# A hybrid decoder step on one core: a different order of row-tile turns and squares ahead of the first products, and query latents on 520 columns

## The reference, cut to what matters

```python
xn = rmsnorm(h, g_norm)                       # 536 rows x 2048
proj = xn @ w_in                              # 2048 -> 4416
u, zs, cq, ckv, kpe, za = split(proj)         # 1024, 1024, 768, 512, 64, 1024
ssm_out = glu(gelu(ssm_scan(u) + d * u)) * silu(zs)
q = rmsnorm(cq, g_qn) @ w_uq                  # query latent -> 8 heads of 128 + 64
c, k_pe = rmsnorm(ckv, g_kvn), rope(kpe)      # stored for all 536 rows
o = attention(q, c, k_pe)                     # prompt: causal; samples: 2048 paged keys each
h = h + concat(ssm_out, o * silu(za)) @ w_out
y = rmsnorm(h, g_final)[16:]                  # the meta rows are dropped
```

## Time and profile before

| what | us |
|---|---|
| timed runs: lowest, median, highest | 1114.28, 1118.61, 1121.12 |
| the profiled execution | 1112.71 |
| its span, first to last instruction | 1111.0 |
| TensorE busy in it | 1040.4 (94%) |
| granted TensorE clock, mean over the span | 0.976 |

### The profile page before, as it was taken

One profiled execution on the slowest core, in us unless ns is written; L12 is line 12 of the kernel. 1 busy time (PEld: TensorE's weight loads), 2 busy tenths in 40 slices (PEclk: granted clock), 3 DMA queues, 4 the chain that ended last, 5 costly groups with the idle time before them and its releaser, 6 DMA issues.

```text
span 1111.0 us, 26974 instructions
## 1 busy us (share of the span) xinstructions
PE 1040.4 (94%) x10653; PEld 961.2 (87%) x10653; DVE 627.1 (56%) x1348; ACT 376.6 (34%) x783; POOL 159.0 (14%) x257
## 2 busy tenths in 40 slices
PE   6799999999999999999999989888799899999995
PEld 5699999999999999998899987665565569999995
DVE  5467264544286656659795527578789733323332
ACT  6521211122124221134652221455446423223333
POOL 0002230000050000010340720304344200000000
PEclk8799999999999999999999999889999999999998
DMA  9435843331353433243645774748998894332213
GB/s 258 102 99 128 168 122 91 96 96 52 96 163 105 136 102 114 86 141 98 218 140 155 235 227 155 229 152 259 288 296 283 265 299 130 91 98 76 80 34 154
DMA packets 201772, 169.90 MB, mean 153 GB/s; under 512 B 37547, under 2 KB 166054, under 8 KB 200102
## 3 DMA queue, kind: packets, MB, share of 16 engines
q1 hardware_dynamic: 178566, 119.12, 38.1%
q0 software_dynamic: 11616, 29.11, 8.7%
q10 hardware_dynamic: 11496, 20.36, 5.1%
HBM read 140.89 MB, written 25.31 MB: 150 GB/s over the span
## 4 chain that ended last, share of the span: by engine, by line
PE 80%; ACT 7%; DVE 4%; issue 4%; DMA 3%; SPq 1%; ACTq 0%; POOL 0%; DVEq 0%; POOLq 0%
PE gemm L2126 13%; PE gemm L2127 13%; PE gemm L2128 13%; PE gemm L2494 6%; PE gemm L2496 6%; PE gemm L2495 6%; PE misc L2398 2%; PE gemm L2413 2%; PE misc L2202 2%; PE gemm L2443 1%; PE misc L2212 1%; PE misc L2153 1%; PE gemm L2332 1%; PE gemm L2334 1%; PE gemm L2333 1%
## 5 line engine op out<-in xcount | busy, mean ns | idle before, releaser
L2126 PE MATMUL gemm<-xh,w_hi 128*128 128x260 f32 (+2 forms) x1056 | 302.2, 286 | 0.0
L2127 PE MATMUL gemm<-xl,w_hi 128*128 128x260 f32 (+2 forms) x1056 | 300.7, 285 | 0.0
L2128 PE MATMUL gemm<-xh,w_lo 128*128 128x260 f32 (+2 forms) x1056 | 299.9, 284 | 0.0
L1321 DVE TENSOR_TENSOR w_lo<-w_raw,w_hi 128x2048 fp32r<-128x2048 f32 (+3 forms) x63 | 110.6, 1756 | 159.1 <-ACT w_hi L861 157.1
L861 ACT ACTIVATE w_hi<-w_raw 128x2048 fp32r<-128x2048 f32 (+3 forms) x63 | 90.7, 1439 | 321.8 <-PE gemm L2128 280.5
L2126 PEld LDWEIGHTS gemm<-xh,w_hi 128*128 128x128 f32 x1056 | 198.8, 188 | 0.7
L2128 PEld LDWEIGHTS gemm<-xh,w_lo 128*128 128x128 f32 x1056 | 199.1, 189 | 0.0
L2127 PEld LDWEIGHTS gemm<-xl,w_hi 128*128 128x128 f32 x1056 | 198.9, 188 | 0.0
L2494 PE MATMUL gemm<-comb_hi,w_hi 128*128 128x260 f32 x512 | 147.7, 288 | 1.2 <-DVE comb_lo L1984 1.1
L2496 PE MATMUL gemm<-comb_hi,w_lo 128*128 128x260 f32 x512 | 145.5, 284 | 0.0
L2495 PE MATMUL gemm<-comb_lo,w_hi 128*128 128x260 f32 x512 | 145.5, 284 | 0.0
(11 more groups left out here) (397 smaller groups left out, 1994.1 us busy)
## 6 DMA issues: line engine op xcount, KB each, us to landing
w_raw<-w_in SPq DMA_DIRECT2D x35, 1024.0 KB, 6.3
ckv<-cache_ckv POOLq DMA_DIRECT2D x76, 256.0 KB, 3.8
w_raw<-w_out SPq DMA_DIRECT2D x16, 1024.0 KB, 5.8
ckv<-cache_ckv SPq DMA_DIRECT2D x52, 256.0 KB, 3.6
z_d<-ev ACTq DMA_DIRECT2D x16, 260.0 KB, 2.1
w_raw<-w_glu SPq DMA_DIRECT2D x8, 512.0 KB, 4.2
yt<-x_prompt SPq DMA_DIRECT2D x4, 1024.0 KB
o_y_p<-yt SPq DMA_DIRECT2D x4, 1024.0 KB
```

What stands on the lines that cost most here:

```text
L1321: dve.tensor_tensor(w_lo[:, slot, 0:width], w_raw[:, slot, 0:width], w_hi[:, slot, 0:width].bitcast(F32), ALU.subtract).then_inc(w_lo_read ...
L2126: pe.matmul(acc, a, xa, start=k == 0, stop=False)
L2127: pe.matmul(acc, a, xb, start=False, stop=False)
L2128: last = pe.matmul(acc, b, xa, start=False, stop=k == k_tiles - 1)
```

## The change

1. **Tile 4 on its own.** The 24 rows of tile 4 are loaded before tiles 2 and 3 and turned as one group (group 8) of sixteen small transposes into one bank. A new function `x_last` makes both parts on VectorE in three operations on 384 columns. Tiles 2 and 3 are groups 9 to 16, four k-tiles each; their high parts are made by ScalarE, the low parts by VectorE.
2. **Turns between products.** Groups 8 to 14 stand before k = 1, 3, ..., 13 of half 0 of block 1, groups 15 and 16 behind it. Half 1 of block 0 has no turns inside.
3. **Squares.** Tile 3 is squared by VectorE (one operation with a running sum, in place, after its last `xl`), tiles 2 and 4 by ScalarE after its last `xh`.
4. **Factors later.** The spreading products stand inside half 1 of block 1, between k = 5 and k = 6.
5. **Query latents on 520 columns.** The six query blocks of B_LAT use OWN; the copies, the stores, the load back, squares, sums, scaling and splits leave the 16 meta columns out. The loops of ScalarE and VectorE around them are cut in two or written out.
6. **Page groups 4 and 5** wait for gemm_done to reach B_V instead of B_K.

```diff
-X_GROUPS = [(t, k, 4) for t in range(3) for k in range(0, KD, 4)] + [(3, k, min(3, KD - k)) for k in range(0, KD, 3)]
+X_GROUPS = [(t, k) for t in (0, 1) for k in range(0, KD, 4)] + [(4, 0)] + [(t, k) for t in (2, 3) for k in range(0, KD, 4)]
+X_DONE = [4 * g + 4 if g < 8 else 4 * g + 3 for g in range(len(X_GROUPS))]
...
+            sp.dma_start(xtok[0:N_META, 4, :], x_prompt[4 * P - N_META:SEQ, :]).then_inc(x_loaded[2], 16)
+            sp.dma_start(xtok[N_META:N_META + N_SAMPLE, 4, :], x_sample).then_inc(x_loaded[2], 16)
             for t in (2, 3):
...
-            pool.wait_ge(gemm_done, B_K)
+            pool.wait_ge(gemm_done, B_V)
             for i in (4, 5):
                 load_pages(pool, i, (0, 1), 0)
...
-            square(0)
-            square(1)
-            act.wait_ge(xh_done, 48)
-            x_high(range(12, len(X_GROUPS)))
-            for t in (2, 3, 4):
-                square(t)
+            square(0, 0)
+            square(1, 1)
+            x_high(range(9, 17))
+            square(2, 2)
+            square(4, 3)
...
+            def x_last():
+                rows = TILES[4][1]
+                turned = misc[0][:, 0:KD * rows].rearrange("p (k t) -> p k t", k=KD)
+                gain = vecs[:, GN:GN + KD].unsqueeze(2).to_broadcast([P, KD, rows])
+                dve.wait_ge(xt_ready, 9)
+                dve.tensor_tensor(turned, turned, gain, ALU.mult).then_inc(xl_done, 1)
+                dve.wait_ge(xl_done, 33)
+                dve.tensor_copy(xh[:, :, 4 * P:T], turned).then_inc(xl_done, 1)
+                dve.wait_ge(xl_done, 34)
+                dve.tensor_tensor(xl[:, :, 4 * P:T], turned, xh[:, :, 4 * P:T].bitcast(F32), ALU.subtract).then_inc(xl_done, 1)
...
-            x_low(range(8, 12), high_too=True)
-            x_low(range(12, len(X_GROUPS)))
+            x_last()
+            x_low(range(9, 17))
+            dve.scalar_tensor_tensor(out=xtok[:, 3], in0=xtok[:, 3], scalar=1.0, in1=xtok[:, 3], op0=ALU.mult, op1=ALU.mult,
+                                     accum_out=stat[:, 3:4]).then_inc(xl_done, 1)
...
-                for h, (h0, hw) in enumerate(HALVES):
+                    for h, (h0, hw) in enumerate(halves):
+            copy_query, copy_key = copy_out(OWN), copy_out(HALVES)
...
             pe.wait_ge(w_lo_ready, 2)
             for k in range(KD):
-                if k in (3, 6, 9, 12):
-                    turn_x((8 + (k - 3) // 3,))
+                if k % 2 and k < 15:
+                    turn_x((8 + k // 2,))
                 first_half(1, 1, 0, (k,))
-            turn_x(range(12, 16))
-            for k in range(KD):
-                if k in (3, 6):
-                    turn_x((16 + (k - 3) // 3,))
-                last = first_half(0, 0, 1, (k,), 3 * KD)
-            last.then_inc(gemm_done, 1)
-            pe.wait_ge(x_scaled, 5)
-            pe.wait_ge(xl_done, 4 * KD)
-            for t in range(5):
...
-            first_half(1, 1, 1, range(KD)).then_inc(gemm_done, 1)
+            turn_x((15, 16))
+            first_half(0, 0, 1, range(KD), 51).then_inc(gemm_done, 1)
+            first_half(1, 1, 1, range(0, 6))
+            spread_factors()
+            first_half(1, 1, 1, range(6, KD)).then_inc(gemm_done, 1)
...
-                multiply(n, n % 2, KD, xh, xl, lambda b=b: chunk_sums(b))
+                multiply(n, n % 2, KD, xh, xl, lambda b=b: chunk_sums(b), halves=OWN if b < 4 else HALVES)
```

More of the change, by code:

```diff
@@ L392, in blocks, with with_first_pass @@
                 body(n, n // 2, n % 2, n + 2 if n + 2 < B_OUT or B_OUT <= n < B_END - 2 else None)
-        def with_first_pass(eng, body, first_pass):
+        def with_first_pass(eng, body, late, first_pass):
             for n in (B_LAT, B_LAT + 1):
                 body(n, n // 2, n % 2, B_LAT)
[L398 to L403, removed]
+            for first in (0, 4):
+                with eng.Fori(0, 2) as i:
+                    for u in range(2):
+                        n = B_LAT + 2 + first + u
+                        first_pass(i * 2 + (first + u))
+                        (body if first == 0 else late)(i * 2 + n, i + n // 2, n % 2, B_LAT)
+            late(B_LAT + 10, (B_LAT + 10) // 2, B_LAT % 2, B_LAT)
         bias_glu = vecs[:, 10:18]
@@ L410, in build, with lat_cols @@
         KPE_OUT = (d["o_kpe_p"].rearrange("l b t r -> (l b t) r"), d["o_kpe_s"].rearrange("l b t r -> (l b t) r"))
+        def lat_cols(k):
+            return slice(N_META if k < 6 else 0, T)
         def gate_count(n, r, slot):
@@ L841, in _, with square @@
         def _(act):
-            def square(t):
+            def square(t, before):
                 rows = TILES[t][1]
@@ L1522, in _ @@
             for n in (B_LAT, B_LAT + 1):
[L1523 to L1524 removed]
+                copy_query(n, n // 2, n % 2, B_LAT)
+            with dve.Fori(0, 2) as i:
                 for u in range(2):
@@ L2052, in turn_x @@
                     else:
-                        pe.wait_ge(x_loaded[t], (32, 16, 16, 48)[t])
+                        pe.wait_ge(x_loaded[min(t, 6 - t)], (32, 16, 48, 16, 48)[t])
                     if g >= 4:
                         pe.wait_ge(xl_done, X_DONE[g - 4])
-                    for i in range(kw):
-                        cols = slice((k0 + i) * P, (k0 + i + 1) * P)
-                        last = pe.transpose(misc[g % 4][:, i * width:i * width + P], xtok[:, t, cols], ident[:])
-                        if t == 3:
-                            rows = width - P
-                            last = pe.transpose(misc[g % 4][:, i * width + P:(i + 1) * width], xtok[0:rows, 4, cols], ident[0:rows, 0:rows])
+                    rows = TILES[t][1]
+                    for i in range(KD if t == 4 else 4):
+                        last = pe.transpose(misc[g % 4][:, i * rows:(i + 1) * rows], xtok[0:rows, t, (k0 + i) * P:(k0 + i + 1) * P],
+                                            ident[0:rows, 0:rows])
                     last.then_inc(xt_ready, 1)
@@ L2073, in first_half, with spread_factors @@
                 return last
+            def spread_factors():
+                pe.wait_ge(x_scaled, 5)
+                for t in range(5):
+                    rows = TILES[t][1]
+                    out = misc[0][:, t * P:(t + 1) * P] if t < 4 else misc[1][:, 0:rows]
+                    last = pe.matmul(out, ones[0:rows, :], diag[0:rows, t, 0:rows], start=True, stop=True)
+                last.then_inc(prep_t_ready, 1)
             turn_x(range(0, 8))
@@ L2080, in _ @@
             for k in range(KD):
-                if k in (3, 6, 9, 12):
-                    turn_x((8 + (k - 3) // 3,))
+                if k % 2 and k < 15:
+                    turn_x((8 + k // 2,))
                 first_half(1, 1, 0, (k,))
-            turn_x(range(12, 16))
-            for k in range(KD):
-                if k in (3, 6):
-                    turn_x((16 + (k - 3) // 3,))
-                last = first_half(0, 0, 1, (k,), 3 * KD)
-            last.then_inc(gemm_done, 1)
-            pe.wait_ge(x_scaled, 5)
-            pe.wait_ge(xl_done, 4 * KD)
-            for t in range(5):
-                rows = TILES[t][1]
-                out = misc[0][:, t * P:(t + 1) * P] if t < 4 else misc[1][:, 0:rows]
-                last = pe.matmul(out, ones[0:rows, :], diag[0:rows, t, 0:rows], start=True, stop=True)
-            last.then_inc(prep_t_ready, 1)
-            first_half(1, 1, 1, range(KD)).then_inc(gemm_done, 1)
+            turn_x((15, 16))
[3 more added lines that the diff above has]
+            first_half(1, 1, 1, range(6, KD)).then_inc(gemm_done, 1)
             pe.wait_ge(prep_t_read, 3)
```

110 lines of the change are left out of this document (51 added, 59 removed).

## The result

| | before | after |
|---|---|---|
| timed runs, median us (lowest to highest) | 1116.81 (1114.28 to 1121.12) | 1096.88 (1094.34 to 1104.86) |
| the profiled execution, us | 1112.71 | 1097.7 |
| its span, us | 1111.0 | 1095.6 |

The ratio is 0.984 (95% interval 0.980 to 0.988), which is 17.8 us less; the two medians are 19.9 us apart. The median of 1096.88 us lies in the range of the forecast, 0.9 us above its lower end. The same kernel timed again later gave 1095.08 us against 1114.17 for the kernel before, 0.981 (0.978 to 0.985). Its two profiled executions took 1097.7 and 1096.9 us.

The account below looks back on a forecast made before the run. TensorE, busy 1040.4 of 1111.0 us, was taken as the bound, gains coming from its stalls, slow clock or columns. Gains 12.5 + 2.0 + 2.2 = 16.7 us: profiled 1112.7 to 1096.0, median 5.9 above, 1101.9; range 1096 to 1110.

Parts of the forecast that it names:

- a start without its slow clock and its long wait: From block 0, half 0 to block 2: 26.9 us instead of 39.41, so block 2 starts at 52.5, 12.5 us earlier.
- shorter query blocks: Query latents: six blocks go from 11.87 to 11.53 us each, 2.0 us gained.
- key weights without page loads beside them: Key blocks: the 6.11 us load takes about 3.06 and the idle 2.22 us goes; 2.2 us gained, bounds 0 to 3.05.
- the turn of four: Start, TensorE: four transposes of one group cost 0.44 us, eight such groups 3.52.
- the factors: Start: after the squares and a 3.41 us rest of the chain, the row factors are ready at 45.7.
- the wait for them: Before the spreading products: TensorE arrives at 44.6 and waits 1.1 us, where it waited 5.56.
- the spreading products: Inside half 1 of block 1: 1.28 us at the upper clock, half of 2.56; 2.56 if they don't follow the clock.
- the rival of the weights: Start: block 2 waits for its weights, or the factors are late; TensorE waits 1.5 to 2.4 us, 1103.9; chance 0.12.
- 0.6 us of cover, and more gain at the start would find this wait: Before block 2: its weights' load, high part, low part and copies are done at 51.9, against its start at 52.5.
- The rival with 0.15: Start: the clock falls between the turns, 7 us at half speed costing 3.5 us, up to 10; 1108.9; chance 0.15.
- wrong if a later stage waits for something that doesn't move with TensorE: Whole kernel: one sign of a wrong prediction; the other was a start gaining less than 8 us.
- 3.4 us of scatter: Range of the timed median: the runs shown differ by 6.8 us, so 3.4 was allowed to each side.

Follow-up runs that it names:

- loads-first kernels: Changed kernel, weight loads of blocks 2 and 3 ahead of the `cnat` loads, spreading at k = 9: 1095.31 us, 0.983; with page groups 4, 5 moved back: 1097.06, 0.986.
- pages only: Kernel before with one edit: page groups 4 and 5 wait for gemm_done to reach B_V instead of B_K; 1113.41 us, ratio 0.999.
- doubled turns: Changed kernel with groups 9 to 16 turned twice over, the second turn writing the same values; 1112.7 us in one run.
- shapes sorted: Kernel before, in each group of tiles 3 and 4 the 128-row transposes first, then the 24-row ones; 1111.61 us, ratio 0.998.
- factors early: Changed kernel with the spreading products back ahead of all of half 1 of block 1; 1110.66 us in one run.

## Why the prediction was right

Forecast were 1101.9 us in a range of 1096 to 1110; measured are 1096.88. The three mechanisms (a start without its slow clock and its long wait, shorter query blocks, key weights without page loads beside them) are each seen in a run. Their sizes came out at 12.6, 1.5 and 0.6 us in the profiled pair, against 12.5, 2.0 and 2.2.

**The start.** Block 2 was forecast at 52.5 and started at 52.45. Term by term, forecast against profile: the turn of four 0.44 against 1.14 - 6 x 0.118 = 0.43; group 8 1.3 against 1.10; half 1 of block 0 from 36.1 against 35.50; `x_last` 1.8 against 1.75; ScalarE's last square 42.3 against 41.51; the factors 45.7 against 44.9, and the wait for them 1.1 against 0.68; the spreading products 1.28 against 1.41. TensorE was 0.7 us ahead of the forecast behind them, and lost most of it to the next bound: the weights of block 2, whose followers I had at 51.9 and the profile has at 52.30 (51.18 + 1.12, the last copy behind it). Without that hold block 2 would have started at 52.02 (the transposes of `cnat` at 51.23, and 0.79). So the agreement to 0.1 us is partly luck: TensorE's own path was 0.5 us shorter than forecast and the load's path 0.4 longer, and the idle 0.19 us for `ev` is the sign that I had given for the rival of the weights. The step "0.6 us of cover, and more gain at the start would find this wait" is the one that the loads-first kernels and the second profile of the changed kernel bear out.

**The start before.** The 12.5 us were measured against one execution. Another execution of the same instructions (pages only) came to block 4's row at 73.77, not 77.24. Of these 3.5 us it was 0.8 ahead at the end of half 0 of block 0 already (24.84 against 25.63), and the other 2.7 lie where the clock was 0.53 in the one and 1.00 in the other. Against such an execution the start gives 9.1 us. My reading took the stretch at 0.53 for a fixed part of the kernel. That did no harm for the profiled pair, but the gain of the start is a range, 9 to 12.6 us.

**The clock between the turns.** The rival with 0.15 did not come. Behind 5.1 us of transposes alone the clock was 0.53 in one execution and 1.00 in another (pages only); with doubled turns it stayed at 1.00. The instructions up to there are the same in the two kernels before, so what decides whether the clock falls is open. Where TensorE had stood still for 3.0 us and more before the spreading products, it was low behind them in all four profiles (before, pages only, shapes sorted, factors early). The Trainium skill, "TensorE: Matmul & The Clock Gate", part 4 (PE-mode transpose), says that transposes don't count as busy for the clock as matmuls do; the first of these executions fits it, the second and the doubled turns don't show it, so it bore no price here.

**The query latents.** 2.0 us forecast, 1.5 in the profiled pair and 1.7 over all profiles. What I left out is that the loads of the first chunk step do not move with TensorE: in one of two profiles they took 0.2 us back. I had looked for such places only where the trace of before already showed a wait. By my own words ("wrong if a later stage waits for something that doesn't move with TensorE") that wait is a sign against the prediction; it is worth 0.2 us in the pair and up to 1.0 in other kernels. The other 0.1 to 0.3 us are within what the stretch differs between two profiles of one kernel (509.05 and 508.27).

**The pages.** 2.2 forecast, 0.6 in the profiled pair, 2.7 over all profiles of the key blocks. The step that failed in the pair was to treat one load as the stage: page group 2, which did not move, ran beside a w_uk load in the changed profile, and that load took 4.75 us. The chain of waits of the changed kernel:

```profile
617.06 4.75 DMA w_raw<-w_uk
```

The load ahead of the slow one in the earlier trace rows had taken 3.06. TensorE's wait of 2.22 us was gone, shorter ones stood elsewhere: its waits for `wuk_t` between 590 and 680 us went from 3.1 us in total to 1.7, and to 0.6 in the second profile. Which load is beside which page group changes between executions. The mechanism is shown in both directions by the fifth load; its size is an average.

**The sum.** 16.7 forecast, 15.0 between the profiled executions (1112.71 to 1097.7); by the timed runs 17.8 by their ratio and 19.9 between the medians, and 20.8 and 19.1 in the second timing. The median came out at 1096.88, 5.0 below the forecast of 1101.9, though the profiled execution came out 1.7 above its own forecast of 1096.0. The difference is the 5.9 us between the profiled execution of the kernel before and its median, which I carried over to the changed kernel, whose profiled execution was 0.8 above its median: 5.9 + 0.8 - 1.7 = 5.0. That step had no row behind it. In the comparison the kernel before stood at 1116.81 and not at 1118.61, so 1.8 of the 5.9 were the draw of three runs. Without the 3.4 us of scatter the range would have ended at 1099.5, and the median would lie outside it; that it lies inside owes as much to that allowance as to the terms.

The terms from the profiles (9.1 to 12.6, 1.7, 2.7) add up to 13.5 to 17.0, and the timed gain is above that. What makes it wider is not settled. It is not that one kernel scatters more than the other: thirty timed executions of the kernel before, run beside these experiments, took 1107.98 to 1121.94 us, ten of the changed kernel 1091.12 to 1104.86. A lead, not shown, is the clock. Among the thirty, the mean granted clock was 0.977 to 0.980 in the six that took less than 1110.1 us and 0.970 to 0.972 in the five above 1120; the medians of the clock are 0.974 for the thirty and 0.9835 for the ten. An estimate that takes span times (1 less clock) as the time lost to the clock gives 6.9 us of difference for the profiled pair (0.976 and 0.982) and 10.9 for the medians. In which stretch a timed execution loses it no run shows, since only one execution of the kernel before has a trace.

**The chances.** I gave 0.82 to faster. By the same paragraph a third of the clock's 0.15 belongs there too, which makes 0.87; the forecast's time and range do not hang on it.

## What to carry to other kernels

Walk the critical engine instruction by instruction up to the next thing that it must wait for, with prices from the same trace, and then ask for each other engine and each load when it would be ready at that new time: here that gave the new start to 0.1 us, two errors of 0.4 to 0.5 us cancelling, and named the bound that took over. Where a stage's length depends on the clock or on which transfers meet, one profile of before is one draw; take its neighbour stretches from several executions before a term is sized. And when work moves forward, list the loads that do not move with it, also those behind which nothing waits yet.

## What the runs showed of the hardware

- Transposes of different heights in turn cost more than sorted ones: a pair of a 128-row and a 24-row transpose 0.43 us, in groups of three alike 0.24 to 0.26, sixteen 24-row ones alone 0.07 each.
- The granted clock fell in one execution (0.53) and not in another (1.00) behind the same 5.1 us of transposes; it stayed at 1.00 with 0.88 us of transposes to 0.71 us of products, and was low behind 3.0 us of standing still (0.73 over the next 6.4 us).
- The stretch with the attention took 250.0 to 264.8 us in the nine kernels that have the same instructions in it; in a slow part of it the clock was 0.81.
- A 256 KB load of key weights took 3.06 us beside one page group and 6.11 beside another in one execution. The fifth of these loads took 5.48 to 7.25 us in five kernels with a page group issued around it and 2.69 to 3.43 in nine without.
